# Strassen's scheme for two of the eight k pairs of the gate and up products in a single-core decoder layer

## What is computed

```python
D_FF = -(-(8 * D_MODEL) // (3 * 256)) * 256
...
def swiglu(h, w_gate, w_up, w_down):
    return (jax.nn.silu(h @ w_gate) * (h @ w_up)) @ w_down
```

## Time and profile before

| what | value |
|---|---|
| median of 3 runs | 1227.99 us (1227.68 to 1228.08) |
| the profiled execution | 1228.24 us, with a span of 1226.4 us |
| mean granted TensorE clock | 0.999 of full speed |
| PE busy | 1216.5 us, 99% of the span |
| PEld busy (under PE's work) | 1010.9 us, 82% |
| DVE busy | 670.3 us, 55% |
| ACT busy | 589.6 us, 48% |
| POOL busy | 81.9 us, 7% |
| DMA | 234.44 MB, 191 GB/s over the span |

### The profile page before, as it was taken

How to read it: one execution, slowest core, us unless ns; L and a number is a source line. 1 busy time by engine, 2 the same in 40 slices (tenths; PEclk the granted TensorE clock), 3 DMA queues, 4 the chain that set the end, 5 groups by cost and what they waited for, 6 DMA issues and landing times.

```text
span 1226.4 us, 16327 instructions
## 1 busy us (share of the span) xinstructions
PE 1216.5 (99%) x5562; PEld 1010.9 (82%) x5562; DVE 670.3 (55%) x798; ACT 589.6 (48%) x758; POOL 81.9 (7%) x89
## 2 busy tenths in 40 slices
PE   9999999999999999999999999999999999999997
PEld 7888888888888888888888888888888888888886
DVE  6655555558755677554454454455455444554444
ACT  6665554546644655644444444444444443434442
POOL 0042422201300000000000000000000000000000
PEclk9999999999999999999999999999999999999999
DMA  9755555556555554565555555555655565656563
GB/s 362 275 189 177 170 168 179 179 175 218 174 184 176 171 175 153 187 224 190 188 187 192 188 188 193 186 184 187 199 187 185 180 204 170 212 181 210 180 202 118
DMA packets 65700, 234.44 MB, mean 191 GB/s; under 512 B 7680, under 2 KB 8448, under 8 KB 65280
## 3 DMA queue, kind: packets, MB, share of 16 engines
q1 hardware_dynamic: 62928, 225.60, 55.6%
q10 hardware_dynamic: 2736, 8.35, 1.8%
HBM read 231.83 MB, written 2.10 MB: 191 GB/s over the span
## 4 chain that ended last, share of the span: by engine, by line
PE 99%; issue 0%; ACT 0%; POOL 0%; DVE 0%; POOLq 0%; DVEq 0%
PE ps L379 31%; PE ps L381 31%; PE ps L380 31%; PE ps L410 1%; PE ps L417 0%; PE ps L491 0%; PE ps L446 0%; PE ps L451 0%; PE ps L575 0%; PE ps L499 0%; PE ps L457 0%; PE ps L597 0%; PE ps L463 0%; PE ps L464 0%; PE ps L450 0%
## 5 line engine op out<-in xcount | busy, mean ns | idle before, releaser
L989 DVE TENSOR_TENSOR wlo<-raw,whi 128x1024 fp32r<-128x1024 f32 x422 | 519.5, 1233 | 452.1 <-ACT whi L672 450.8
L672 ACT ACTIVATE whi<-raw 128x1024 fp32r<-128x1024 f32 x422 | 446.4, 1059 | 476.8 <-PE ps L381 464.2
L379 PE MATMUL ps<-whi,ahi 128*128 128x512 f32 x864 | 338.3, 392 | 0.0
L381 PE MATMUL ps<-whi,alo 128*128 128x512 f32 x864 | 336.4, 389 | 0.0
L380 PE MATMUL ps<-wlo,ahi 128*128 128x512 f32 x864 | 336.2, 389 | 0.0
L381 PEld LDWEIGHTS ps<-whi,alo 128*128 128x128 f32 x864 | 162.2, 188 | 33.9
L380 PEld LDWEIGHTS ps<-wlo,ahi 128*128 128x128 f32 x864 | 162.3, 188 | 33.0
L379 PEld LDWEIGHTS ps<-whi,ahi 128*128 128x128 f32 x864 | 162.2, 188 | 32.9
L379 PE MATMUL ps<-whi,bhi 128*128 128x512 f32 x448 | 180.1, 402 | 0.0
L381 PE MATMUL ps<-whi,blo 128*128 128x512 f32 x448 | 175.1, 391 | 0.0
L380 PE MATMUL ps<-wlo,bhi 128*128 128x512 f32 x448 | 174.4, 389 | 0.0
(11 more groups left out here) (178 smaller groups left out, 584.8 us busy)
## 6 DMA issues: line engine op xcount, KB each, us to landing
raw<-w_stream SPq DMA_DIRECT2D x423, 512.0 KB, 3.3
res<-x_in ACTq DMA_DIRECT2D x4, 512.0 KB, 7.7
stage<-mem_in ACTq DMA_DIRECT2D x4, 512.0 KB, 7.2
proj<-mem_T ACTq DMA_DIRECT2D x2, 1024.0 KB, 7.8
stage<-x_T SPq DMA_DIRECT2D x7, 256.0 KB, 6.1
y_out<-yout SPq DMA_DIRECT2D x4, 320.0 KB, 3.0
gfin<-g_final ACTq DMA_DIRECT2D x1, 1024.0 KB, 8.3
y_out<-yout ACTq DMA_DIRECT2D x4, 192.0 KB, 3.2
```

Source lines behind the costliest of these rows:

```text
L379: nc.tensor.matmul(bank, lhsT=a_h, rhs=w_h, start=start, stop=False)
L381: return nc.tensor.matmul(bank, lhsT=a_l, rhs=w_h, start=False, stop=stop)
L672: nc.scalar.activation(tile_pair(whi, j), tile_pair(raw, j), ACT.Copy).then_inc(hi_ready, 1)
L989: vec.tensor_tensor(tile_pair(wlo, j), tile_pair(raw, j), tile_pair(whi, j).bitcast(f32), ALU.subtract).then_inc(lo_ready, 1)
```

## The change

The activations of one k pair form 2 x 2 blocks of 128 x 128 (token tile by k block), and the gate and up weights of the same k pair form 2 x 2 blocks of 128 x 512 (k block by gate or up). Their product has eight block products of three matmuls. For the k pairs 0 and 1 of each chunk (a "quad" each) the change uses Strassen's scheme in Winograd's form: seven block products, of which some take sums of blocks as factors.

- **Order.** A chunk now has 20 places p instead of 16 steps: gate pairs 2, 3, 4 at p 0 to 2, a quad in four parts at p 3 to 6, gate pairs 5, 6, 7 at p 7 to 9, the other quad at p 10 to 13, up pairs 2 to 7 at p 14 to 19. Part 0 of a quad has 3 matmuls, parts 1 to 3 have 6 each. The weight stream is stored in this order; a quad takes two tiles of it, (b11, b21) and (b12, b22).
- **Weight sums.** DVE makes them in the raw slots: `b12 - b11` and `b22 - (b12 - b11)` in part 0 (512 columns each), and both halves of the first tile less that sum in part 1 (1024). ACT casts the changed tiles again in parts 2 and 3, where it waits for `w_sums`. So four casts and splits stand for a quad (the first of half width), where there were four.
- **Raw slots.** `RAW_DONE` says after which split each raw slot may be loaded again; both tiles of a quad are held until the splits of its parts 2 and 3.
- **Activation sums.** `s_forms` makes four sums for each quad once, at the start of chunk 0, in five DVE operations; ACT and DVE split them into `sfh` and `sfl`.
- **Banks.** Products P1, P5, P6, P7 of the two quads collect in banks 4 to 7. ACT copies bank 4 into `uu` behind cast 15 (`p1_copy`); DVE adds the gate banks and the four together in six operations of 512 columns behind split 16 (`combine`); silu is made from SBUF behind cast 19 (`gate`); and `up` adds `uu` before it multiplies. The transposes of `fact` move from step 3 to p 18.
- The load of `gfin` moves from the start of the second chunk to the start of the down product, and the two square sums of chunk 0 from step 2 to p 6 and 8.

The core of the diff:

```diff
+QUADS = 2
+QUAD_PARTS = 4
+QUAD_AT = (3, 10)
+CHUNK_RAW = 2 * SPG
+CHUNK = CHUNK_RAW + QUADS * (QUAD_PARTS - 2)
+GATE_STEPS = {0: 2, 1: 3, 2: 4, 7: 5, 8: 6, 9: 7}
+UP_STEPS = {14 + n: QUADS + n for n in range(SPG - QUADS)}
+RAW_DONE = (1, 2, 3, 7, 6, 8, 9, 10, 14, 13, 15, 16, 17, 18, 19, 20)
...
+P1_AT, COMBINED, SILU_AT, UNITS_AT = 13, 14, 17, 18
...
+        def chunk_place(c, p):
+            c, p = c + p // CHUNK, p % CHUNK
+            v = J_FF + c * CHUNK + p
+            for n, at in enumerate(QUAD_AT):
+                if at <= p < at + QUAD_PARTS:
+                    return v, J_FF + c * CHUNK_RAW + at - 2 * n, QUADS * c + n, p - at
+            before = sum(p >= at + QUAD_PARTS for at in QUAD_AT)
+            return v, J_FF + c * CHUNK_RAW + p - 2 * before, None, None
...
+            with sp.Fori(0, NFC) as ci:
+                for n in range(CHUNK_RAW):
+                    done = RAW_DONE[n - RING] - (CHUNK if n < RING else 0)
+                    sp.wait_ge(lo_ready, ci * CHUNK + (J_FF + done))
+                    sp.dma_start(tile_pair(raw, n), stream[ci * CHUNK_RAW + (J_FF + n)]).then_inc(w_loaded[n % RING], 16)
...
+            def product(bank, a, w, start, stop):
+                nc.tensor.matmul(ps[:, bank, :], lhsT=a[0], rhs=w[0], start=start, stop=False)
+                nc.tensor.matmul(ps[:, bank, :], lhsT=a[0], rhs=w[1], start=False, stop=False)
+                return nc.tensor.matmul(ps[:, bank, :], lhsT=a[1], rhs=w[0], start=False, stop=stop)
...
+            def quad_part(c, ci, n, part):
+                v = J_FF + c * CHUNK + QUAD_AT[n] + part
+                opens, closes = n == 0, n == QUADS - 1
+                left, right = ([b[:, v % RING, half * GC:(half + 1) * GC] for b in (whi, wlo)] for half in range(2))
+                def a_block(t, k):
+                    return [b[:, KS * n + k, t * P:(t + 1) * P] for b in (ahi, alo)]
+                def s_form(f):
+                    return [b[:, f, n, :] for b in (sfh, sfl)]
+                pe.wait_ge(lo_ready, ci * CHUNK + (v + 1))
+                if part == 0:
+                    done = product(up_banks[0], s_form(3), right, opens, False)
+                if part == 1:
+                    done = product(gate_banks[0], a_block(0, 1), right, False, closes)
+                    if closes:
+                        done.then_inc(tile0_done, 1)
+                    done = product(4, a_block(0, 0), left, opens, closes)
+                if part == 2:
+                    product(5, s_form(0), left, opens, closes)
+                    done = product(6, s_form(1), right, opens, closes)
+                if part == 3:
+                    product(7, s_form(2), left, opens, closes)
+                    done = product(gate_banks[1], a_block(1, 1), right, False, closes)
+                done.then_inc(step_used, 1)
...
+            def quad(c, ci, n):
...
+                    bank_free(G_FF + 2 * c + 1, ci)
+                    if c == 0:
+                        pe.wait_ge(s_lo, 1)
+                        pe.wait_ge(unit_lo, U_FF)
+                    else:
+                        pe.wait_ge(unit_lo, ci * 2 + (U_FF + 2 * (c - 1)))
...
             def chunk(c, ci=0):
...
+                    if c == 0 and p == 1:
+                        await_out(pe, G_FF - 1)
...
+                    if c == 1 and p == UNITS_AT:
+                        await_out(pe, G_FF + 2, ci)
+                        ffn_unit(0, ci)
+                        ffn_unit(1, ci)
...
+            def chunk_cast(c, p, ci=0):
...
+                if part is None or part == 0:
+                    act.wait_ge(w_loaded[j % RING], loaded_by(j, raw_it))
+                if part == 0:
+                    act.wait_ge(w_loaded[(j + 1) % RING], loaded_by(j + 1, raw_it))
+                if part in (2, 3):
+                    act.wait_ge(w_sums, ci * (3 * QUADS) + (3 * q + part))
+                if part in (0, 2):
+                    src = tile_pair(raw, j + 1)
+                if part == 0:
+                    whi_here, src = whi_here[:, GC:KS * GC], src[:, GC:KS * GC]
+                act.wait_ge(step_used, ci * CHUNK + (v - RING + 1))
+                nc.scalar.activation(whi_here, src, ACT.Copy).then_inc(hi_ready, 1)
...
+            def p1_copy(c, ci=0):
+                act.wait_ge(step_used, ci * CHUNK + (J_FF + c * CHUNK + QUAD_AT[-1] + 2))
+                if c:
+                    await_out(act, G_FF + 2 * c - 1, ci)
+                nc.scalar.activation(uu[:, 0, :], ps[:, 4, :], ACT.Copy).then_inc(p1_copied, 1)
...
             def gate(c, ci=0):
...
+                await_out(act, G_FF + 2 * c, ci)
...
+                for t in range(TT):
+                    done = nc.scalar.activation(silu[:, t, :], silu[:, t, :], ACT.Silu, scale=rstd[:, 3, t:t + 1])
...
+            for p in range(CHUNK):
...
+                if p == 0:
+                    act.wait_ge(s_made, 1)
+                    nc.scalar.activation(sfh[:].rearrange("p f n m -> p (f n m)"), fact[:].rearrange("p t n -> p (t n)"),
+                                         ACT.Copy).then_inc(s_hi, 1)
...
+                if p == P1_AT:
+                    p1_copy(0)
+                if p == SILU_AT:
                     gate(0)
...
             def up(c, ci=0):
...
+                dve.wait_ge(silu_ready, ci + (c + 1))
+                dve.wait_ge(combined, ci * 4 + (4 * c + 4))
...
-                    done = vec.scalar_tensor_tensor(fact[:, t, :], ps[:, 2 * ((G_FF + 1) % 2) + t, :], rstd[:, 3, t:t + 1],
...
+                    vec.tensor_tensor(fact[:, t, :], ps[:, 2 * ((G_FF + 1) % 2) + t, :], uu[:, t, :],
+                                      ALU.add).then_inc(up_sums, 1)
+                    dve.wait_ge(up_sums, ci * TT + (TT * c + t + 1))
+                    done = vec.scalar_tensor_tensor(fact[:, t, :], fact[:, t, :], rstd[:, 3, t:t + 1],
                                                     silu[:, t, :], ALU.mult, ALU.mult)
...
+            def combine(c, ci=0):
+                gate_bank = 2 * (G_FF % 2)
+                p5, p6, p7 = (ps[:, bank, :] for bank in (5, 6, 7))
+                base = 4 * c
+                dve.wait_ge(p1_copied, ci + (c + 1))
+                dve.wait_ge(step_used, ci * CHUNK + (J_FF + c * CHUNK + QUAD_AT[-1] + QUAD_PARTS))
+                vec.tensor_tensor(silu[:, 0, :], ps[:, gate_bank, :], uu[:, 0, :], ALU.add)
+                vec.tensor_tensor(uu[:, 0, :], p6, uu[:, 0, :], ALU.add).then_inc(combined, 1)
+                dve.wait_ge(combined, ci * 4 + (base + 1))
+                vec.tensor_tensor(uu[:, 1, :], p7, uu[:, 0, :], ALU.add).then_inc(combined, 1)
+                vec.tensor_tensor(uu[:, 0, :], p5, uu[:, 0, :], ALU.add).then_inc(combined, 1)
+                dve.wait_ge(combined, ci * 4 + (base + 2))
+                vec.tensor_tensor(silu[:, 1, :], ps[:, gate_bank + 1, :], uu[:, 1, :],
+                                  ALU.add).then_inc(evacuated[G_FF % 2], 1)
+                vec.tensor_tensor(uu[:, 1, :], p5, uu[:, 1, :], ALU.add).then_inc(combined, 1)
...
+            def chunk_split(c, p, ci=0):
...
+                dve.wait_ge(hi_ready, ci * CHUNK + (v + 1))
+                if part == 0:
+                    vec.tensor_tensor(b12, b12, b11, ALU.subtract).then_inc(w_sums, 1)
+                    src = b22
+                if part == 2:
+                    src = b12_b22
+                vec.tensor_tensor(lo_here, src, hi_here.bitcast(f32), ALU.subtract).then_inc(lo_ready, 1)
+                if part == 0:
+                    dve.wait_ge(w_sums, sums + (3 * q + 1))
+                    vec.tensor_tensor(b22, b22, b12, ALU.subtract).then_inc(w_sums, 1)
+                if part == 1:
+                    dve.wait_ge(w_sums, sums + (3 * q + 2))
+                    both = b11_b21.rearrange("p (h n) -> p h n", h=2)
+                    vec.tensor_tensor(both, both, b22.unsqueeze(1).to_broadcast([P, 2, GC]),
+                                      ALU.subtract).then_inc(w_sums, 1)
+            def s_forms():
...
+                first = slice(0, KS * QUADS)
+                vec.tensor_tensor(a_raw, ahi[:, first, :].rearrange("p k t -> p (k t)").bitcast(f32),
+                                  alo[:, first, :].rearrange("p k t -> p (k t)").bitcast(f32), ALU.add).then_inc(s_raw, 1)
...
+                vec.tensor_tensor(forms[:, 0], a21, a22, ALU.add).then_inc(s_sums, 1)
+                vec.tensor_tensor(forms[:, 2], a21, a11, ALU.subtract)
+                dve.wait_ge(s_sums, 1)
+                vec.tensor_tensor(forms[:, 1], forms[:, 0], a11, ALU.subtract).then_inc(s_sums, 1)
+                dve.wait_ge(s_sums, 2)
+                vec.tensor_tensor(forms[:, 3], a12, forms[:, 1], ALU.subtract).then_inc(s_made, 1)
...
+            for p in range(CHUNK):
+                chunk_split(0, p + LEAD)
+                if p == 0:
                     add_group(G_FF - 1, J_FF)
-                if s == 1:
+                    s_forms()
+                if p == 1:
```

(46 more changed lines are left out.)

119 lines of the change are left out of this document (76 added, 43 removed).

## The result

The changed kernel takes 1242.4 us (median of 4 runs, 1239.67 to 1243.31) against 1227.84 (1227.66 to 1228.08) for the kernel before in the same runs: a ratio of 1.0115, with an interval of 1.0102 to 1.0127. It is 14.6 us slower, with 66 matmuls fewer. The profiled execution took 1242.53 us, with a span of 1240.7 and a granted clock of 0.999.

The account below looks back on a forecast made before the run. PE was taken as the bound, busy for 99% of the span. Terms: -14.96 + 3.4 + 1.8 + 11 x 1.2 = +3.4 us on the profiled 1228.24, so 1231.7; 1231.4 as a median, range 1219 to 1245.

Parts of the forecast that it names:

- The saving: Gate quads of all 11 chunks: 66 matmuls fewer at 0.2267 us each, 14.96 us less.
- the chain of a steady chunk: Order of loads, casts, splits and PE's matmuls in one chunk: 43.09 us without waits, plus 1.2 of wait.
- the landing of the grouped loads: Second quad's second tile, third of three close loads: lands 6.2 us behind the first issue, between 5.8 and 6.8.
- no spare: Second quad, p 12 and p 13: splits end at 23.1 and 24.3, PE wants them at 23.12 and 24.48.
- third rival: Loads of a group slow one another or land in 4.2 us; p 11 and p 12 wait too: s = 2.5, 1246, chance 0.24.
- The wait at p 17: Split 17, behind `combine` on DVE, ends at 35.1; PE wants it at 34.00: about 1.2 us a chunk.
- s: PE's wait at p 12 and p 17 in one chunk: taken as 1.2 us, forecast case 0.7 to 1.6.
- Chunk 0: First chunk's extra waits: 3.4 us at the first quad (activation sums), 1.8 at the second (second square sum).
- DVE's overlap: Short DVE operations in `combine` and part 0 start 0.60 us apart; the rival without overlap, 0.69 each, 1239, chance 0.03.
- DVE and ACT as bounds: Throughput in a chunk: DVE about 34 of 43 us, ACT less; neither becomes a bound by its load.
- The clock: Sign of going wrong: the granted clock, 0.999 before the change, drops when PE waits.
- The second rival: Waits are small as grouped loads land at the full rate: s = 0.4, 1222.6, or 1218 without p 17's; chance 0.27.

Follow-up runs that it names:

- swapped loads: The changed kernel with SP issuing the load of stream tile 8 of a chunk before that of tile 7: 1229.81 us, ratio 1.0016.
- half loads: The changed kernel with each gate and up chunk load bringing only 512 of a tile's 1024 columns, so the output is not the layer's: 1217.41 us, ratio 0.9915.

## Why the prediction came out as it did

- **Direction right, size short.** 1231.4 us was forecast and 1242.4 measured, inside the range of 1219 to 1245 and near its upper end. The change was forecast as +3.4 us and came out as +14.6, four times as much; it is the width of the range that held it.
- **The saving**: -14.96 forecast, -15.0 measured by itself.
- **Up to the group of loads** the chain of a steady chunk was right. SP issues gate tile 7 at 731.12, 10.86 on the chunk's clock, as forecast, and the quad's second tile 1.3 us later (1.1 forecast).
- **The step that failed is the landing of the grouped loads**: "the third 5.8 us" from below, 6.8 from above, "I take 6.2". It was 7.3 in the chunk above, 7.0 on the median of the ten, and at or over the upper bound in nine of them. The lower bound spread the loads at the full rate behind the first, 1.28 us each; the two that follow the first took 3.6 us together (median), not 2.6. In the chunk above the tile stood at 18.1 instead of 17.1 on the clock; parts 1 and 2 are late and PE loses 1.3 us there, 1.1 on the mean of the ten chunks, where the sum had nothing. The chain behind the landing was right, and its finding of no spare too: by the table above, PE's wait would be 0.1 to 0.3 us at the 6.2 that was taken. The run with the swapped loads, which brought that tile back to 17.0 or less, took the wait away in all later chunks but one. The prediction had named this as a sign that it goes wrong: a third load that lands other than 6.2 us behind the first issue. This is the third rival, and its 1246 was nearer than the forecast.
- **The wait at p 17**: 1.2 us a chunk was forecast, from `combine` ahead of split 17. Moving `combine` gave back 1.07 by the chunks and 13.0 / 11 = 1.2 by the times, which hold chunk 0 as well. So s is 1.1 + 1.1, measured as 45.32 - 43.09 = 2.2. The chain there was late as a whole: the load for p 16 is issued at 25.7 on the clock (24.5 forecast), lands 3.4 us later, as taken, and `combine` begins at 31.5 (30.1). PE came later too, by its wait at the quad, so the price stayed.
- **Chunk 0** was about right. Its weight loads waited 2.38, 0.43 and 1.04 at the first quad (forecast 2.0, 0.55, 0.85), 2.04 and 1.04 at the second (0.9, 0.9) and 0.95 at p 17 (1.2), each with the 0.15 in it that costs nothing. From PE's first step to the first `up` sum it took 49.89 us (539.30 - 489.41), before 44.13 (533.94 - 489.81, 1.36 of it for the six matmuls): 7.1 us of waits, 6.4 forecast. Both causes were shown: the first quad's by the sums on GpSimd, the second's, in the traces of the kernel with these sums, by the later square sum. The swapped loads left the second's at 2.09 and 1.04, but in chunk 0 they did not bring the tile: it landed at 512.9, behind 512.4 in the changed kernel, and ACT waited 2.0 and 2.9 us for it before the cast of part 0. So in the changed kernel the landing may have a share in these waits beside the square sum; the split between the two was not measured. The first wait is only 0.92 with `combine` later. There the granted clock was 0.50 from 502 to 504 us, behind the stands at the first quad, and PE itself came later; in the changed kernel and with the swapped loads it was 1.00 there, and the waits are 2.04 and 2.09.
- **The sum again**: -15.0, 7.1 for chunk 0 and 10 x 2.23 for the others give +14.4; +14.6 was measured.
- **DVE's overlap** held: `combine`'s operations of 0.68 start 0.60 apart where nothing is waited for (753.69 to 754.29, 754.29 to 754.89). The Trainium skill's "VectorE: DVE Perf Modes", section "The DRAIN you can't avoid", says what the prediction took from it, and adds that "A next op that is not held starts earlier". These rows agree with the addition; the prediction left it out.
- **DVE and ACT as bounds**: neither, as forecast. With half loads the chunks ran at 43.15.
- **The clock** stayed at 0.999.
- **The second rival**, small waits, rested on the sustained rate of the earlier trace rows and on the fit of the Trainium skill's "DMA: Bandwidth & Descriptors", section "Anatomy of one DMA — SWDGE (gpsimd) path". The page gives that fit for transfers issued from GpSimd; here SP issues them. The first load of a close group keeps near to it, 3.1 to 3.7 us; the second and third do not.

## What to carry to other kernels

When a change makes buffers come free in bursts, price each load by its place in the burst, not by a lone load and the sustained rate; and look whether a load whose buffer is free stands in the queue behind one whose buffer is not. Work added to a helper engine costs by where it stands: six short operations cost 1.1 us a chunk on an engine that was busy for 173.5 of 226.6 us, because a split queued behind them while the tile ahead of them had landed late; two positions later they cost nothing. Before moving work earlier on the same engine, read that engine's idle time there; the same work on an idle engine gave the gain that the move on DVE had spent.
